# Two transformer blocks on one core: a third tile in the first loop, and a new order of heads, softmax and weight halves

## The reference, cut to what matters

```
s = q.k/8 + (cum_t - cum_s)        # fox; cum = cumsum(log_sigmoid(gate)), causal, softmax, @ v
p = softmax(s1 + alibi) - lam * softmax(s2 + alibi)                  # diff, then @ v and an RMS norm
x = x + g1 * (mixed @ w_out);  x = x + g2 * (silu(h2 @ w_gate) * (h2 @ w_up)) @ w_down
```

## Time and profile before

| | |
|---|---|
| median of the runs | 817.07 us |
| the profiled execution | 818.92 us, of it span 817.2 us |
| PE busy | 775.0 us, 95% of the span |
| PE weight loads | 616.8 us, 75% |
| DVE busy | 466.4 us, 57% |
| ACT busy | 390.6 us, 48% |
| POOL busy | 59.4 us |
| read from HBM | 156.99 MB |

### The profile page before, as it was taken

How to read it: one execution, slowest core, us unless ns; L and a number is a source line. 1 busy time by engine, 2 the same in 40 slices (tenths; PEclk the granted TensorE clock), 3 DMA queues, 4 the chain that set the end, 5 groups by cost and what they waited for, 6 DMA issues and landing times.

```text
span 817.2 us, 10224 instructions
## 1 busy us (share of the span) xinstructions
PE 775.0 (95%) x3955; PEld 616.8 (75%) x3955; DVE 466.4 (57%) x607; ACT 390.6 (48%) x544; POOL 59.4 (7%) x70
## 2 busy tenths in 40 slices
PE   3988899988999999999999999999999999999995
PEld 2667675656888889888878887777888888888884
DVE  3466676747565556464595436555565656545364
ACT  3255666644344334353634356665455545335252
POOL 2004030010000000000280000000010000000001
PEclk9999999999999999999999999999999999999998
DMA  9998336895655347656749464333565645564601
GB/s 275 289 361 274 112 105 254 312 397 195 219 194 184 125 155 232 232 180 203 255 162 331 155 205 154 105 104 111 170 194 162 200 156 201 164 201 154 206 26 51
DMA packets 86785, 158.73 MB, mean 194 GB/s; under 512 B 5226, under 2 KB 23875, under 8 KB 84690
## 3 DMA queue, kind: packets, MB, share of 16 engines
q1 hardware_dynamic: 84562, 151.16, 55.7%
q0 software_dynamic: 2128, 6.90, 2.7%
q10 hardware_dynamic: 48, 0.01, 0.0%
HBM read 156.99 MB, written 1.08 MB: 193 GB/s over the span
## 4 chain that ended last, share of the span: by engine, by line
PE 82%; DVE 5%; issue 3%; SPq 3%; ACT 3%; DMA 2%; POOL 1%; DVEq 0%; POOLq 0%; ACTq 0%
PE PS L872 25%; PE PS L874 24%; PE PS L873 24%; PE PS L986 3%; DMA raw<-in_w_ada 2%; PE PS L1066 1%; ACT whi L1165 1%; PE PS L960 1%; DVE wlo L1377 1%; PE PS L1037 1%; SPq L802 1%; PE PS L1092 1%; PE PS L1021 1%; SPq L790 1%; POOL hrs L1780 1%
## 5 line engine op out<-in xcount | busy, mean ns | idle before, releaser
L1377 DVE TENSOR_TENSOR wlo<-raw,whi 128x2048 fp32r<-128x2048 f32 (+1 forms) x126 | 280.2, 2226 | 190.4 <-ACT whi L1165 162.4
L1165 ACT ACTIVATE whi<-raw 128x2048 fp32r<-128x2048 f32 (+1 forms) x126 | 227.1, 1804 | 156.2 <-PE PS L874 156.2
L872 PE MATMUL PS<-whi,hT 128*128 128x512 f32 (+1 forms) x704 | 280.6, 399 | 2.2 <-issue 1.9
L874 PE MATMUL PS<-whi,hT 128*128 128x512 f32 (+1 forms) x704 | 272.8, 388 | 0.0
L873 PE MATMUL PS<-wlo,hT 128*128 128x512 f32 (+1 forms) x704 | 272.7, 387 | 0.0
L872 PEld LDWEIGHTS PS<-whi,hT 128*128 128x128 f32 x704 | 133.5, 190 | 33.1 <-issue 8.4
L874 PEld LDWEIGHTS PS<-whi,hT 128*128 128x128 f32 x704 | 133.3, 189 | 27.5
L873 PEld LDWEIGHTS PS<-wlo,hT 128*128 128x128 f32 x704 | 133.7, 190 | 23.9
L872 PE MATMUL PS<-whi,hidT 128*128 128x512 f32 x216 | 84.5, 391 | 0.0
L874 PE MATMUL PS<-whi,hidT 128*128 128x512 f32 x216 | 84.1, 389 | 0.0
L873 PE MATMUL PS<-wlo,hidT 128*128 128x512 f32 x216 | 84.1, 389 | 0.0
(11 more groups left out here) (227 smaller groups left out, 643.7 us busy)
## 6 DMA issues: line engine op xcount, KB each, us to landing
raw<-in_w_in SPq DMA_DIRECT2D x36, 1024.0 KB, 5.1
raw<-in_w_ff SPq DMA_DIRECT2D x32, 1024.0 KB, 5.2
raw<-in_w_ada SPq DMA_DIRECT2D x16, 1024.0 KB, 6.9
raw<-in_w_gate SPq DMA_DIRECT2D x10, 1024.0 KB, 5.4
raw<-in_w_up SPq DMA_DIRECT2D x10, 1024.0 KB, 5.1
raw<-in_w_down SPq DMA_DIRECT2D x10, 1024.0 KB, 5.2
raw<-in_w_ada SPq DMA_DIRECT2D x16, 512.0 KB, 7.2
raw<-in_w_out SPq DMA_DIRECT2D x8, 1024.0 KB, 5.1
```

The source lines that it names most:

```text
L872: pe.matmul(o, ah, wh, start=(k == 0), stop=False)
L874: return pe.matmul(o, al, wh, start=False, stop=end)
L1165: act.activation(split_view(whi, i), slab_view(raw, slot, i), ACT.Copy).then_inc(hi_made, 1)
L1377: dve.tensor_tensor(split_view(wlo, i), slab_view(raw, slot, i), whole(split_view(whi, i)), ALU.subtract).then_inc(lo_made, 1)
```

## The change

The first loop takes three fox tiles for each chunk (slabs of 768 KB; the third tile in PSUM banks 4 and 5), with a tile's banks computed anew. The gate's product and its sums come first behind the loop. The query's part of the forget bias (`cum`, `cumq`, `mcum`) is gone: it is a constant along a softmax row.

In attention `scores` is cut into `scores` (maxima), `exp` (ACT) and `probs` (DVE's inverse sums and scaling), and `heads(u+2)` stands right behind `scores(u+1)`, ahead of both. `split` is now ACT's high half alone; the low half is a step of its own, `lower`. Between the first and the last `scores` of a run of pairs the high half stands behind `values`, and the low half behind `probs`, or ahead of the slab's own first piece where it has not come yet. `diffnorm` is done in two halves. `norm 1` takes the root for each row tile, DVE makes a diagonal matrix `diag` of it, and PE multiplies x by it in place of transposing a scaled copy. Two small loads go from SP's queue to ACT's. The `ada` loads start later in the list, one at a time.

```diff
-BETWEEN = {"fox": (2, 1, 1, 2, 2), 1: (2, 1, 1, 2, 1), 2: (2, 1, 1, 1, 1), 3: (2, 0, 1, 1, 1),
-           "diff": (2, 0, 1, 0, 1), 7: (1, 0, 1, 0, 1),
-           "moba": (2, 0, 1, 0, 1), 8: (2, 0, 1, 0, 0), 15: (2, 1, 1, 0, 1)}
+BETWEEN = {"fox": (2, 1, 1, 1), 3: (1, 1, 1, 1), "diff": (1, 1, 0, 1), 7: (1, 0, 0, 1),
+           "moba": (2, 1, 0, 1), 8: (2, 1, 0, 0), 15: (2, 2, 0, 1)}
...
             if u != us[-1]:
                 out += [("scores", u + 1)]
+            if u + 2 <= us[-1]:
+                out += [("heads", u + 2)]
+            if u != us[-1]:
+                out += [("exp", u + 1), ("probs", u + 1)]
             if moba and u != us[0]:
                 out += [("back", u - 1)]
-            out += fill(c[0]) + [("probsT", (u, 0))] + ([("probsT", (u, 1))] if moba else []) + fill(c[1])
-            if u + 2 <= us[-1]:
-                out += [("heads", u + 2)]
-            out += fill(c[2])
+            out += fill(c[0]) + [("probsT", (u, 0))]
+            if moba:
+                out += [("probsT", (u, 1))]
+            out += fill(c[1])
             if kind_of(u) == "fox":
-                out += [("probsT", (u, 1))] + fill(c[3])
-            out += [("values", u)] + fill(c[4])
+                out += [("probsT", (u, 1))] + fill(c[2])
+            out += [("values", u)] + fill(c[3])
+            if u == FOX_P + 2:
+                out += [("diffnorm", 0)]
+            if u == FOX_P + 3:
+                out += [("diffnorm", 1)] + turns("diff", 0, (0,))
...
     for j in range(KC):
-        slabs.append(dict(weight="w_in", row=j * P, chunks=1, col=0, cols=2 * W))
+        slabs.append(dict(weight="w_in", row=j * P, chunks=1, col=0, cols=3 * W))
+        step = [("piece", dict(T=fox[n], k=j, slab=j, off=n * W, first=n == 0, last=n == 2)) for n in range(3)]
+        if j < KC - 1:
+            order += rows(j + 1) + step[:1] + [("xT", j + 1), ("col", j + 1), *early, ("part0", j + 1)]
+            order += step[1:] if j < KC - 2 else step[1:2] + early + step[2:]
+            order += {KC - 4: [("setup", 0), ("lam", 0)], KC - 2: [("relbias", 0)]}.get(j, [])
         else:
+            order += step[:1] + early + [("evac", fox[0])] + step[1:2] + [("evac", fox[1]), ("vectors", 0)]
+            order += step[2:] + [("evac", fox[2])]
+    order += [("fgate", 0), ("logf", 0), ("unit", 0), ("unit", 1)]
...
+    tail = insert(tail, (5, [("heads", 0)]), (6, early), (9, early + [("scores", 0), ("heads", 1), ("exp", 0), ("probs", 0)]),
+                  (11, [("unit", 2)]), (12, [("lam", 1)]), (20, [("unit", 3)]), *[(20 + j, [ada[8 + j]]) for j in range(6)])
...
+    order += [("norm", 1), ("first", 0), ("mod", 2), ("first", 1)]
+    order += turns("norm", 1, (0, 1)) + parts("norm", 1, (0, 1)) + [("first", 2), ("first", 3)]
...
+        if it[0] == "piece" and it[1]["first"] and it[1]["slab"] >= KC + 2:
+            held = tiles[it[1]["T"]]["name"] == "w_out" and it[1]["k"] == 4 and tiles[it[1]["T"]]["n"] == 1
+            split = up_to("split", split, max(wanted, it[1]["slab"] + 1))
+            wanted = it[1]["slab"] + (2 if held else 3)
+            if not paired:
+                split = up_to("split", split, wanted)
+            lower = up_to("lower", lower, it[1]["slab"] + 1 if paired else split)
         out.append(it)
+        if it[0] == "scores":
+            paired = it[1] not in (FOX_P + DIFF_P - 1, PAIRS - 1)
+        if it[0] == "probs":
+            lower = up_to("lower", lower, split)
+        if it[0] == "values":
+            split = up_to("split", split, wanted)
...
+                elif kind == "first":
+                    key = ("norm", 1, i)
+                    b = turn_bank(TURNS[key])
+                    take(b)
+                    pe.wait_ge(diag_made, 1)
+                    for c in range(2):
+                        k = 2 * i + c
+                        pe.matmul(PS[:, b, c * S:c * S + P], x[:, 0, k * P:(k + 1) * P], diag[:, 0, :], start=True, stop=True)
```

More of the change, by code:

```diff
@@ L168, in plan @@
     ada = [("ada", j) for j in range(3 * KC)]
-    fox = [tile("fox", n, KC, "h") for n in range(2)]
-    def column(j):
-        return [("col", j), ("part0", j)]
+    fox = [tile("fox", n, KC, "h") for n in range(3)]
     def rows(j):
@@ L180, in plan @@
     early = [("split", None)]
-    order += [("cond", 0), ("chunk", 0), ("sums0", 0), ("norm", 0), ("rows", 0), ("early", 0), *early, ("xT", 0), *column(0)]
-    order += [*rows(1), ("xT", 1), *early, *column(1)]
+    order += [("cond", 0), ("chunk", 0), ("sums0", 0), ("norm", 0), ("rows", 0), ("early", 0), ("xT", 0), ("col", 0), *early,
+              ("part0", 0)]
     for j in range(KC):
-        slabs.append(dict(weight="w_in", row=j * P, chunks=1, col=0, cols=2 * W))
[L185 to L191, removed]
-        else:
[L193 to L196, removed]
+        slabs.append(dict(weight="w_in", row=j * P, chunks=1, col=0, cols=3 * W))
[4 more added lines that the diff above has]
+            order += {KC - 4: [("setup", 0), ("lam", 0)], KC - 2: [("relbias", 0)]}.get(j, [])
+        else:
+            order += step[:1] + early + [("evac", fox[0])] + step[1:2] + [("evac", fox[1]), ("vectors", 0)]
+            order += step[2:] + [("evac", fox[2])]
+    order += [("fgate", 0), ("logf", 0), ("unit", 0), ("unit", 1)]
     tail = []
@@ L230, in plan @@
                 m = FOX_P + DIFF_P
-                now = insert(now, (0, [("heads", m)]), (3, [("scores", m), ("heads", m + 1)]))
+                now = insert(now, (0, [("heads", m)]), (3, [("scores", m), ("heads", m + 1), ("exp", m), ("probs", m)]))
             order += now
@@ L613, in home @@
         def home(s):
-            return (s // 2 % SPL, s % 2) if s < KC else ((s - KC // 2) % SPL, 0)
+            return s % SPL
         def split_view(t, s):
-            slot, half = home(s)
-            return t[:, slot, half * 2 * W:half * 2 * W + SLABS[s]["chunks"] * SLABS[s]["cols"]]
+            return t[:, home(s), 0:SLABS[s]["chunks"] * SLABS[s]["cols"]]
         def slabs_under(s):
-            slot, half = home(s)
-            under = [e for e in range(s) if home(e)[0] == slot and (e >= KC or s >= KC or home(e)[1] == half)]
-            return under[-1] + 1 if under else 0
+            return max(0, s - SPL + 1)
         def landed(eng, it):
@@ L861, in _ @@
                         pe.wait_ge(lo_made, s + 1)
-                    if k == 0 and T >= 2:
-                        for ready in tile_readers(T - 2):
+                    if k == 0 and tile_under(T) >= 0:
+                        for ready in tile_readers(tile_under(T)):
                             pe.wait_ge(*ready)
+                    if (T, k) == (2, 0):
+                        take(4, 5)
                     operand_ready(T, k)
@@ L982, in _ @@
                         pe.wait_ge(s, v)
[L983 to L986, removed]
+                    if is_affine(i):
+                        for c in range(2):
+                            last = pe.matmul(PS[:, b, c * S + P:(c + 1) * S], src[:, 1, c * P:(c + 1) * P], diag[:, 1, :],
+                                             start=True, stop=True)
+                    else:
+                        for c in range(2):
+                            for t in range(TB):
+                                o = c * S + t * P
+                                last = pe.transpose(PS[:, b, o:o + P], src[:, t, c * P:(c + 1) * P], ident)
                     last.then_inc(turned, 1)
@@ L1195, in _ @@
                     squares(*i)
-                elif kind == "norm" and i < 2:
-                    act.wait_ge(norm_rs, i + 1)
-                    act.activation((xn1, xnb)[i][:, 0, :], x[:, 0, :], ACT.Copy, scale=nrs[:, i, 0:1]).then_inc(xn_act, 1)
+                elif kind == "norm" and i == 0:
+                    act.wait_ge(norm_rs, 1)
+                    act.activation(xn1[:, 0, :], x[:, 0, :], ACT.Copy, scale=nrs[:, 0, 0:1]).then_inc(xn_act, 1)
                 elif kind == "part" or kind == "turn" and not is_affine(i):
@@ L1811, in _ @@
                     n = i
+                    if n == 1:
+                        for t in range(TB):
+                            pool.wait_ge(sums_made, 3 + t)
+                            then(pool.tensor_tensor(nss[:, 1, t:t + 1, 0], nss[:, 1, t:t + 1, 0], nss[:, 1, t:t + 1, 1], ALU.add))
+                            last = inverse_root(nrs[:, 1, t:t + 1], nss[:, 1, t:t + 1, 0], D)
+                            last.then_inc(rs1_made, 1)
+                        continue
                     if n:
```

185 lines of the change are left out of this document (88 added, 97 removed).

## The result

The changed kernel took 840.83 us (median of four runs, 837.65 to 843.61) against 817.86 for the kernel before: a ratio of 1.0281, with an interval of 1.0238 to 1.0323. The forecast was 843, range 812 to 856. The profiled execution took 843.61 us, its span 841.9.

What follows compares the result with a forecast made beforehand. PE was taken as the bound, busy 775 of 817 us, with DMA pacing the first loop. 818.92 + 27.8 (second attention) - 1.2 (front part) = 845.5, less 1.85 for the median: 843.7, given as 843, range 812 to 856.

Steps and rivals of the forecast that it cites:

- Moba: Second attention: new PE waits of 18.2 us at scores 10 to 15 plus 10.8 of lost clock; costs 27.8 us.
- Lead of the loop: First loop with three tiles: diff 0 starts at 69.1 instead of 81.52, a lead of 10.2 us.
- the two paces: First loop, time per step: PE 6.0 us, DMA 6.4 us; both put the last chunk at about 55 us.
- Fox waits: First attention: PE waits 3.0 at heads 0, 3.9 at scores 1, 4.7 at piece d2.k0, each plus 1.9 of clock.
- The ends of attention one and ada: End of first attention through norm 1: 4.1 us gained; ada loads waiting for buffers: 3 us lost.
- the front part: Everything ahead of the second attention: 1.2 us gained in sum, bounds 15 gained to 9 lost.
- No low half in front of L1650: Rival, second attention: no low half delays the bank's release, and perhaps likewise in fox; 802 us, chance 0.17.
- The clock stays up: Rival, second attention: waits of 2.4 and 2.5 us come but don't lower the clock; 832 us, chance 0.13.
- POOL's slow scaling: Fox chain: scaling beside DVE's work would make the second unit up to 1.7 us later, time 845; forecast took 0.21.
- Fox does worse: Rival, first attention: each new wait 3 us longer as POOL and DVE meet; 852 us, chance 0.07 for fox or loop.
- it does not do what it says: Rival, first loop: third tile finds no room, loop ends 6 us later; 849 us, chance 0.07 for fox or loop.

Runs made afterwards that it cites:

- moba_as_before: Changed kernel with the second attention put back in its old order, front part left changed: 817.13 us, ratio 0.9990 against the kernel before.
- low75_too: Changed kernel with the second attention's low half behind back, and slab 75's low half ahead of scores 10: 819.94 us, ratio 1.0010 against the kernel before.

## Why the prediction was right, step by step

**Moba, the term that decided (predicted 27.8).** The mechanism held: `lower` between `probs` and `back`, L1674 late, 2.5 us at each of scores 11 to 14 (measured 2.55 to 2.56), 2.4 at scores 15 (2.17). Two sizes were off. At scores 10 I had 5.8 and it was 3.53 + 0.24: the piece of slab 75 waited, and L1674 was ready almost as soon as PE had done it. And the clock fell behind five of the six waits, not behind the last; with a fall at 1.53 us that is 7.7, where I had 10.8. Waits 16.2 + clock 7.7 - old waits 1.2 = 22.7. By the two traces the stretch from heads 8 to PE's L1124 behind the last pair lost 22.4, by the runs 23.8.

**Lead of the loop (predicted 10.2).** 81.52 - 70.54 - 2.2 = 8.8 in the profiled execution. The missing 1.4 is a fall of the clock within the loop, 0.83 over 30 to 40 us. In four of the experiments, with the same loop, it stayed at 1.00 and the last chunk came at 54.12 to 54.97, as the "about 55" had it. Of the two paces the one of PE is right: from 38.5 us on a step takes 6.0 us in every profile, as I had it. DMA's 6.4 didn't come: it moved 338 GB/s from 38.5 to 56.6 us, above the 325 that I had used.

**Fox waits (predicted 3.0 + 3.9 + 4.7, each + 1.9).** Measured 1.95 + 3.45 + 4.32, the last two within half a microsecond and at the places named. The clock fell at all three. By the windows of 4 us above this cost 1.7 to 2.0 each. But behind scores 1 and d2.k0 it stayed down for longer than those windows:

```profile
97.95:99.95 2.00, 2.00 (x6) 1.51 (x6) 1.43 (x5) 2.00 (x10) 0.00 (x0) 0.50 0.00 0
118.99:120.49 1.50, 1.50 (x5) 1.12 (x5) 0.00 (x0) 0.07 (x1) 1.50 (x1) 0.50 0.96 363
```

With these 3.5 us at half clock, half of them lost, the three falls cost 1.7 + 3.0 + 2.8 = 7.5, and waits and clock together 17.2, where I had 17.3. The sum came out by luck: the waits were 1.9 shorter than mine and the clock 1.8 dearer. I had also read the delay wrong, since the clock of the kernel before fell 0.1 to 0.7 us behind its waits' ends and not a microsecond. With two pieces and the 2.2 us of heads and scores set right, the stretch from diff 0 to scores 7 lost 11.3 us, and my terms gave 17.3 - 7.2 = 10.1. The measured ones give 17.2 - 7.2 = 10.0, and waits on ACT's copies of `pt` (1.30 and 0.48), which I hadn't foreseen, make it 11.8.

**The ends of attention one and ada (predicted 4.1 - 3).** The ada waits were 1.40 + 1.47 = 2.9. The wait at the diff transposes fell from 1.89 to 0.46, that at norm 1 from 2.06 to 1.10, and the clock stayed up there. From scores 7 to gate 0 it makes 0.1 gained, in place of 1.1; I haven't traced the rest.

So the front part, predicted at 1.2 gained, lost 2.4 in the profiled execution, and gained 0.8 in the runs of moba_as_before (interval -0.6 to 2.2). The two misses have opposite signs, 3.6 us too good in front and 5.1 us too dear in moba. That 845.5 came so near to 843.61 is luck to that extent. The bounds of my two parts are not what the terms give either: 1.2 + 17.3 = 18.5 gained with no new fox wait, and I had 15; 1.2 - 11.6 = 10.4 lost with each wait doubled, and I had 9.

**The rivals.** *No low half in front of L1650* failed as a description and came true as a kernel: low75_too, at 819.9, and not my 802, since the fox waits are separate from it. *The clock stays up* failed, with 0.50 and 0.57 behind most of the waits. POOL's slow scaling didn't come in the changed kernel (0.20 and 0.21 for the two units); it came in an experiment of mine that put a low half beside it. *Fox does worse* and *it does not do what it says* didn't come: each fox wait was shorter than I had it, and the last chunk came at 56.59, with one fall of the clock in the loop.

## What to carry to other kernels

When one step of a list is cut in two, look on each engine for what the second half now stands in front of. Here one DVE instruction of 2.29 us stood before the one that frees a bank of PSUM, and that cost six waits and five falls of the clock; one step later it left 0.34 us of wait in a pair. A place where its engine waits for another suits such a half, but not when a small operation of POOL is about to start beside it, which then lasts until the half has ended. And a loop that gives 10 us gives them only when every chain that it brings forward has its inputs forward too: the front part with this loop was worth nothing with the three waits in it, and 12 to 14 us with them taken out.

## What the runs showed of the hardware

Over thirteen profiles, behind PE's waits after the first loop: of 54 waits of 0.93 to 1.89 us none was followed by a fall of the granted clock, of 27 waits of 1.93 to 2.72 us 21 were, and at all 18 of 3.43 us and more it fell, at some while PE still waited. At 13 of these 18 it stayed at 0.50 for 6.8 us, at the other five and behind the 21 shorter ones for 3.4 us. I had taken 2.06 as the point from which each wait costs 1.9. In these rows it is 21 cases of 27 up to 2.72 us, at 1.5 us a fall, and what decides it isn't shown: the same 2.18 us went both ways. This is also most of the spread between runs of one kernel. The run of 843.61 us had a mean granted clock of 0.975 and that of 837.65 one of 0.981, which is 5 us of the 6 between them; where hardly any such wait is left the runs lie between 805.04 and 806.63.
